# Unnormalized first chunks behind each norm, with the norm factor applied at the PSUM read, and another order of the attention heads

## The reference

```python
def rms_norm(h, gain):
    h32 = h32 * lax.rsqrt(jnp.mean(h32 * h32, axis=-1, keepdims=True) + EPS)
    return h32 * gain
...
c_act = jax.nn.silu(c)
mod = (c_act @ ada_w[layer] + ada_b[layer])          # shift, scale, gate of each sublayer
h = rms_norm(x, norm_g[layer, 0]) * (1.0 + scale) + shift
x = x + 0.5 * gate * swiglu(h, ffn_w_in[layer, 0], ffn_w_down[layer, 0])
h = rms_norm(x, norm_g[layer, 1]) * (1.0 + scale) + shift
x = x + gate * diff_attention(h, ...)                # layer 1: hgrn2(h, ...)
...
x = x + sliding_window_attention(rmsnorm(x, norm_mix[0]), ...)
x = x + peer_ffn(rmsnorm(x, norm_ffn[0]), ...)       # 16384 experts, product keys
x = x + short_gated_conv(rmsnorm(x, norm_mix[1]), ...)
x = x + peer_ffn(rmsnorm(x, norm_ffn[1]), ...)
```

## Time and profile before

| what | value |
|---|---|
| median of 3 runs | 3052.91 us (3051.86 to 3061.36) |
| the profiled execution | 3055.0 us |
| its span, first to last instruction | 3053.2 us |
| TensorE busy (matmul) | 2964.3 us, 97% |
| DVE busy | 2141.4 us, 70% |
| ACT busy | 1357.4 us, 44% |
| GpSimd busy | 569.8 us, 19% |
| mean granted TensorE clock | 0.987 |

### The profile page before, as it was taken

The page is one execution under the profiler, slowest core; times in us unless marked ns, Lnnn a source line. Parts: engine busy times, 40 slices in busy tenths (PEclk is TensorE's granted clock), DMA queues, the critical chain, the costliest instruction groups (busy, mean ns, idle before and its releaser), DMA issues.

```text
span 3053.2 us, 48385 instructions
## 1 busy us (share of the span) xinstructions
PE 2964.3 (97%) x18778; PEld 2640.5 (86%) x18778; DVE 2141.4 (70%) x3120; ACT 1357.4 (44%) x1486; POOL 569.8 (19%) x311
## 2 busy tenths in 40 slices
PE   5999899999999999999999999999999999999999
PEld 4888788888898887789999988788889999988887
DVE  7787778888766755559967755565859967755565
ACT  4444544454534444444444444444444444444443
POOL 2310313032120210008820000000008830000000
PEclk9999999999999999999999999999999999999999
DMA  7786157777633654145557656676444556655685
GB/s 299 278 284 235 70 207 275 276 269 274 233 112 136 232 171 151 42 145 187 179 200 236 236 197 219 235 280 228 166 180 167 184 199 237 231 206 208 244 288 198
DMA packets 147044, 640.58 MB, mean 210 GB/s; under 512 B 12456, under 2 KB 46416, under 8 KB 90464
## 3 DMA queue, kind: packets, MB, share of 16 engines
q1 hardware_dynamic: 127104, 568.02, 52.3%
q10 hardware_dynamic: 19808, 70.79, 6.3%
HBM read 604.14 MB, written 34.62 MB: 209 GB/s over the span
## 4 chain that ended last, share of the span: by engine, by line
PE 64%; DVE 2%; DMA 1%; ACT 1%; issue 1%; DVEq 0%; ACTq 0%
PE pp L555 10%; PE pp L1139 8%; PE pp L1140 8%; PE pp L1141 8%; PE mz L1205 7%; PE mz L1208 7%; PE mz L1207 7%; PE pp L557 5%; PE mz L1181 2%; DMA raw<-expert_v 1%; ACT w_hi L1268 1%; PE mz L515 1%; PE mz L528 0%; PE pp L1024 0%; DVE w_lo L1774 0%
## 5 line engine op out<-in xcount | busy, mean ns | idle before, releaser
L1774 DVE TENSOR_TENSOR w_lo<-raw,w_hi 128x2048 fp32r<-128x2048 f32 (+1 forms) x416 | 911.5, 2191 | 456.8 <-ACT w_hi L1268 455.9
L1268 ACT ACTIVATE w_hi<-raw 128x2048 fp32r<-128x2048 f32 (+1 forms) x486 | 893.8, 1840 | 513.7 <-DMA raw<-expert_v 362.8
L555 PE MATMUL pp<-hs,w_hi 128*128 128x512 f32 x2272 | 810.1, 401 | 21.6 <-POOL hs L2569 12.8
L557 PE MATMUL pp<-hs,w_lo 128*128 128x256 f32 x2272 | 637.6, 281 | 0.0
L1139 PE MATMUL pp<-hs,w_hi 128*128 128x256 f32 x2048 | 584.8, 286 | 0.0
L1140 PE MATMUL pp<-hs,w_hi 128*128 128x256 f32 x2048 | 579.3, 283 | 0.0
L1141 PE MATMUL pp<-hs,w_lo 128*128 128x256 f32 x2048 | 579.1, 283 | 0.0
L555 PEld LDWEIGHTS pp<-hs,w_hi 128*128 128x128 f32 x2272 | 430.3, 189 | 132.2 <-issue 13.5
L2512 POOL TENSOR_TENSOR w_lo<-raw,w_hi 128x2048 fp32r<-128x2048 f32 x64 | 319.7, 5007 | 1051.6 <-ACT w_hi L1268 1051.5
L557 PEld LDWEIGHTS pp<-hs,w_lo 128*128 128x128 f32 x2272 | 432.1, 190 | 0.9 <-issue 0.7
L1205 PE MATMUL mz<-w_hi,w_split 128*128 128x512 f32 x1024 | 401.2, 392 | 10.2 <-DVE w_split L2345 10.0
(11 more groups left out here) (309 smaller groups left out, 3270.0 us busy)
## 6 DMA issues: line engine op xcount, KB each, us to landing
raw<-expert_u SPq DMA_DIRECT2D x128, 1024.0 KB, 4.8
raw<-expert_v SPq DMA_DIRECT2D x128, 1024.0 KB, 4.8
raw<-ffn_in SPq DMA_DIRECT2D x88, 1024.0 KB, 4.9
ada_raw<-ada ACTq DMA_DIRECT2D x116, 512.0 KB, 5.3
raw<-ffn_down SPq DMA_DIRECT2D x64, 704.0 KB, 5.3
raw<-out_w SPq DMA_DIRECT2D x16, 1024.0 KB, 4.7
raw<-hgrn SPq DMA_DIRECT2D x16, 1024.0 KB, 4.8
raw<-query SPq DMA_DIRECT2D x16, 1024.0 KB, 4.8
```

Of the source, the lines that this page charges most:

```text
L555: mm(outp, w_hi[:, slot, a:a + P], rhs[:, k0 + k].rearrange("p a t -> p (a t)"), start=(k0 + k == 0), stop=False, skip_group_check=True)
L557: last = mm(outp[:, 0:T], w_lo[:, slot, a:a + P], rhs[:, k0 + k, 0, :], start=False, stop=(k0 + k == last_k), skip_group_check=True)
L1268: f(w_hi[:, slot, 0:n], raw[:, slot, 0:n], ACT.Copy).then_inc(hi_ready, 1)
L1774: v.tensor_tensor(w_lo[:, slot, 0:n], raw[:, slot, 0:n], w_hi[:, slot, 0:n].bitcast(F32), ALU.subtract)\
```

## The change

For the norms n = 1 to 9 the first two pairs of chunks (`RAW_PAIRS = 2`, four chunks) are multiplied with x times gain, without the factor 1/rms of the token. The product is multiplied by that factor when it is read from PSUM. So these four chunks do not wait for the norm.

- New operand `xs`, 516 columns a k: [low of x*gain | 2 shift columns | high of x*gain | 2 shift columns]. ACT makes the high part (`raw_high`), DVE the low part (`raw_low`), as soon as each k of x is done; DVE writes the shift columns (`shift_columns`, 8 small linked instructions for n = 1, 4 for the others).
- The raw product has three matmuls for each k where there were two (`raw_part`), of 258, 256 and 258 columns for n below 6, and of 256 each from n = 6 on.
- The first pair (`raw_pair`) is ordered by what is ready behind each kind of sublayer, with `sums` and `spread_norm` between its parts. All `keep_warm` calls of `sums`, the five in `spread_keys` and the three in sliding-window `turn` are gone. The three in `turn` of differential attention stay.
- Reading: `take_raw` on DVE replaces `take_cross` on ACT and `add_halves`. For n below 6 the shift is summed from the two columns first and added afterwards (in the ffn by the silu bias and the product that follow).
- The old `norm` chain (`h32`, `hs` high and low) moves behind: four k after chunk 1 is read and four after chunk 2 (`norm_behind`). The third pair needs `hs`.
- DVE and ACT split both chunks of the second pair before chunk 0 is read.
- `MOD_PLAN` gets a first pair: ffn_in 1 and 2 start one pair later (10 pairs, not 11), ffn_in 3 two pairs later, attention has 4 pairs instead of 3.
- In sliding-window attention step h becomes score(h+2), turn(h), weigh(h-1) on TensorE; weights(h), low(h-2), soft(h+2) on DVE; turned(h), high(h-1), expo(h+2) on ACT.
- Buffers move; `pick_sb` is loaded after the first sliding-window pair on SyncE's queue; the copy to `iota_rep` moves from ffn 0 to the first peer sublayer; the conv taps run three chunks later; the down and out products are unrolled on DVE and ACT.

```diff
+    def raw_part(n, outp, slot, tile0, k):
+        a = (tile0 + k) * P
+        more = 2 if n < 6 else 0
+        wh, wl, x_ = w_hi[:, slot, a:a + P], w_lo[:, slot, a:a + P], xs_of(n, k)
+        mm(outp[:, 0:T + more], wh, x_[:, 0:T + more], start=(k == 0), stop=False, ...)
+        mm(outp[:, 0:T], wh, x_[:, T + 2:2 * T + 2], start=False, stop=False, ...)
+        return mm(outp[:, 0:T + more], wl, x_[:, T + 2:2 * T + 2 + more], start=False, stop=(k == KD - 1), ...)
...
+    def behind_down():
+        late = 1 - half
+        pe.wait_ge(x_done, x0 + KD - 1)
+        for k in range(2): ...            # 6 parts, all tiles but (late, 0)
+        sums(n, KD - 1, KD)
+        pe.wait_ge(x_done, x0 + KD)
+        ...                               # 2 parts, then k = 2 of all 4 tiles
+        spread_norm(n)
+        parts(0, (3,)); parts(1, (3,))
+        for j in range(2):
+            parts(j, range(4, KD)).then_inc(w_used, 1)
+    def behind_out():
+        pe.wait_ge(x_done, x0 + KD - 2)
+        parts(0, range(4)); sums(n, 4, 6); parts(0, (4, 5))
+        pe.wait_ge(x_done, x0 + KD)
+        parts(1, range(2)); sums(n, 6, KD); parts(1, (2, 3))
+        spread_norm(n)
+        parts(1, (4, 5))
+        for j in range(2):
+            parts(j, (6, 7)).then_inc(w_used, 1)
+    def behind_experts():
+        for b in range(4):
+            pe.wait_ge(x_done, x0 + 2 * b + 2)
+            ...                           # k = 2b, 2b+1 of the b tiles already begun
+            if b == 3:
+                sums(n, 0, KD)
+            ...                           # tile b, k = 0 to 2b+1; at b == 3 spread_norm after k == 3
...
     # ACT
+    def norm(n, a, ph):
         for k in range(a, KD, 2):
+            squares(n, k, w)
+            raw_high(n, k) ...
         act.wait_ge(norm_sum, n + 1)
         f(inv_rms[:], mz[:, 0, 0:TB], ACT.Sqrt, ...).then_inc(norm_rms, 1)
+        split_next(ph, 0, ph.pair0, ph.pair0 % 2, ph.pair0 // 2, 0)
+        act.wait_ge(norm_wide, n + 1)
+        f(inv_w[:], mz[:, 0, T:2 * T], ACT.Copy).then_inc(inv_ready, 1)
...
     # DVE
+    def take_raw(ph, n, c, dst):
+        dve.wait_ge(inv_ready, n)
+        dve.wait_ge(w_used, 2 * ph.pair0 + c + 1)
+        if n < 6:
+            link(v.tensor_reduce(shift[:, j], pp[:, j, :, T:T + 2], AX.X, ALU.add))
+        last = v.tensor_tensor(dst, pp[:, j, :, 0:T], inv_w[:].unsqueeze(1).to_broadcast([P, 2, T]), ALU.mult)
+        if n < 6 and ph.kind != "ffn_in":
+            ...                           # two tensor_scalar that add the shift
+        last.then_inc(evac_done, 1)
...
     # sliding-window attention, TensorE
     for h in range(HEADS):
-        turn(h)
         if h + 2 < HEADS:
             score(h + 2)
-        weigh(h)
+        turn(h)
+        if h:
+            weigh(h - 1)
+    weigh(HEADS - 1)
```

More of the change, by code:

```diff
@@ L158, in beyond_plan @@
 def beyond_plan(ph, rp):
-    n = MOD_PLAN[(ph.kind, ph.index)][1]
-    return rp >= n if isinstance(rp, int) else ph.kind == "ffn_in" and n < ph.pairs
+    first, n = MOD_PLAN[(ph.kind, ph.index)][1:]
+    return not first <= rp < first + n if isinstance(rp, int) else ph.kind == "ffn_in" and first + n < ph.pairs
 def each_pair(ph):
@@ L332, in build, with xs_of @@
         one = small[:, 60:61]
+        shift = small[:, 64:68].rearrange("p (j t) -> p j t", j=2)
+        def xs_of(n, k):
+            return xs_1[:, k - 5] if n == 1 and k > 4 else xs[:, k]
         pp = psum("pp", [P, 2, 2, 512])
@@ L561, in first_pair, with raw_tile, normed_tile, wait_k @@
+            def raw_tile(ph, n, rp, pair, half, j, t):
+                for k in range(KD):
+                    last = raw_part(n, pp[:, j, t], 2 * half + j, t * KD, k)
+                return last
+            def normed_tile(n):
+                def wait_k(k):
+                    pe.wait_ge(hs_ready, KD * n + k + 1)
+                return wait_k
             def first_pair(ph, n):
@@ L599, in products @@
                         for t in range(2):
-                            last = tile_product(pp[:, j, t], 2 * half + j, t * KD, hs, 0, KD, KD - 1)
+                            last = raw_tile(ph, n, rp, pair, half, j, t)
+                        last.then_inc(w_used, 1)
+                for rp, pair, half, lap in pairs_of(pe, ph.part(raw, ph.pairs - raw)):
+                    for j in range(2):
+                        pe.wait_ge(lo_ready, 2 * pair + j + 1)
+                        pe.wait_ge(evac_done, ph.evac0 + 2 * rp + j - 1)
+                        first = isinstance(rp, int) and rp == raw and j == 0
+                        for t in range(2):
+                            last = tile_product(pp[:, j, t], 2 * half + j, t * KD, hs, 0, KD, KD - 1,
+                                                normed_tile(n) if first and t == 0 else None)
                         last.then_inc(w_used, 1)
@@ L1352, in ffn @@
                 load_modulation(ph, 0, 0)
-                for rp, pair, half, lap in itertools.chain(pairs_of(act, ph.part(0, 6)), pairs_of(act, ph.part(6, 2))):
+                for rp, pair, half, lap in each_pair(ph):
                     for j in range(2):
@@ L1356, in ffn @@
                         load_modulation(ph, 2 * rp + j + 1, 1 - j)
-                        if j == 0 and not (isinstance(rp, int) and rp == 0):
+                        if j == 0 and rp:
                             squares(n + 1, rp - 1, 1)
+                        if j and rp > 3:
+                            for k in range(2 * rp - 8, 2 * rp - 6) if rp < 7 else (6,):
+                                raw_high(n + 1, k)
             def diff_attention():
@@ L2483, in _ @@
             peer(0, 7)
-            norm(8)
+            norm(8, KD - 2)
             short_conv()
```

494 lines of the change are left out of this document (342 added, 152 removed).

## The result

The changed kernel takes 3037.7 us (median of 6 executions, 3035.4 to 3040.4) where the kernel before, on the same chip, takes 3052.4: a ratio of 0.9941, with a 95% interval of 0.9924 to 0.9957. It is faster, by 15 to 18 us. Timed again in another series it took 3039.2 against 3053.5: 0.9958, 0.9941 to 0.9975. The forecast was 3027.8, range 2998 to 3050: sign and range hold, the gain came out 7 to 10 us smaller. The profiled execution has a span of 3035.2 us against 3053.2, with a mean granted clock of 0.985 against 0.987.

A forecast was written before the change was run, and what follows sets the result against it. TensorE, in work 97% of the span, was taken as the bound. 3055.0 less 18.4 at the norms and 6.7 in the head steps gave 3029.9 profiled, median 3027.8; own range 3012 to 3042, with rivals 2998 to 3050.

The forecast's parts named there:

- Raw products start at once, and take 0.36 a k: At norm boundaries: raw parts start 0.1 us behind the last down product; three matmuls take 0.360 us a k.
- Rival D: Raw products: 258-column matmuls cost more than 256, making the kernel slower, about 3380 us at the float32 fillers' rate; chance 0.08.
- Pair 0 of nine norms, 33.4 net: Last product to end of first raw pair, nine norms: 33.4 us won, with the wait for `take_raw(0)` included.
- Second pair, 3.7: Second raw pair at nine norms: three matmuls a k cost 0.4 us more at each, 3.7 in all.
- VectorE late for the third pair, 10.3: Third pair: TensorE waits on VectorE's queue, 4.5 us at norm 1, 1.9, 1.0, 2.5, 0.4 at norms 2 to 5.
- Head steps, 6.7: Window attention: steps of 4.2 us instead of 6.04 and no first fillers win 13.7, less 7.0 for low clock: 6.7 us.
- the slow steps: Window attention's head steps: two run at 1.2 GHz, about 7.7 us a step, costing 3.5 us more each.
- Rival B: Window attention: the clock stays low through the head steps, giving 3046 us; chance 0.12.
- two more modulation chunks cost 1 later: Differential attention, norm 1: two further chunks with conditioning on VectorE cost 1 us later.
- Rivals A: Norm boundaries and heads: DVE and ACT keep up and the clock returns at once, 2999 us; chance 0.12.
- C: Norm boundaries: DVE's lateness is double what was followed, 22 us more wait, about 3050 us; chance 0.10.
- E: Norm boundaries: the first pair starts no sooner, its operands or `lo_ready` being late, about 3049 us; chance 0.03.

The follow-up runs named there:

- the two fastest: Changed kernel with attention's chunk 6 and 7 tiles behind the head loop, chunk 0 read earlier at norms 7, 8, 9: 3026.5 us; also with convolution taps sooner: 3021.1 us.
- the kernel with the other opcode: Changed kernel with the small add of each conditioning step written as scalar_tensor_tensor instead of tensor_tensor: 3038.7 us against 3052.7 for the kernel before, 0.9951.

## Why the prediction was right, and where it was not

- **Raw products start at once, and take 0.36 a k.** Right. In the first profile the mean step is 0.361 with 258 columns and 0.358 with 256; timeline rows of TensorE after, six steps of the one apart, then ten of the other:

```profile
619.45 0.28 PE L569 MATMUL pp<-xs,w_hi 128*128 128x258 f32 x1
...
621.62 0.28 PE L569 MATMUL pp<-xs,w_hi 128*128 128x258 f32 x1
...
1307.22 0.28 PE L569 MATMUL pp<-xs,w_hi 128*128 128x256 f32 x1
...
1310.80 0.28 PE L569 MATMUL pp<-xs,w_hi 128*128 128x256 f32 x1
```

  Rival D, the dear 258 columns, falls: two columns and an odd start cost 3 ns at most. Against the two-matmul step beside them (0.347 or 0.353) a raw step costs 5 to 14 ns more, so the rows' 13 was a price at the upper end. By the formula that the Trainium skill (TensorE: Matmul & The Clock Gate, Back-to-back issue gap) gives for a matmul in isolation it would be some 3; the traces show more.
- **Pair 0 of nine norms, 33.4 net.** Right: 36.3 and 33.6. The waits for `take_raw(0)` were 1.22, 1.22, 1.09, 1.09 (1.6 forecast) and 3.95 (4.4).
- **Second pair, 3.7.** It lost 4.7 and 5.9. The excess is norm 8, with 2.0 and 3.0 where 0.4 was forecast: behind its wait at chunk 2 the granted clock is 0.50 for part of the pair in both profiles, and it lost only 0.5 in the three kernels whose wait there is 1.75 us or less.
- **VectorE late for the third pair, 10.3.** Right in sum (9.6, 8.6), not norm by norm: norm 1 was given 4.5 and lost 2.4, norm 5 was given 0.4 and lost 1.7.
- **Head steps, 6.7.** Too small by 3 to 4 us. The step at full clock was right (4.24). The term that was mis-sized is that of the slow steps: 5.35 us each in the first profile and not 7.7, so that two cost 2.2 us beyond full speed (3.2 in the second profile) and not 7. Rival B falls too: without any filler the clock is full 0.9 to 3.1 us behind the start of the first `weigh`. Whether `turn` had a part in that, no run here shows.
- **The failed step: "two more modulation chunks cost 1 later".** From chunk 7 on they cost 8.3 us in the first profile and 4.7 in the second. The tiles stood at a place where they delay the keys of the first score; their instructions have both inputs in SBUF and stood still while GpSimd's split ran, which I had not looked at; so TensorE waited 5.35 us, and its clock fell in that wait. The experiments show each of the first two apart. For the clock there is the count of traces only: low in seven of seven with the wait, full in six of six without. How long it stays low is not set by the wait, and makes the difference between 4.7 and 8.3.
- **A step left out.** The taps of the convolution are not in the prediction's sum, nor among what it costed at nothing. Three of them moved into the chunks with the gating: 2.1 us of waits.
- **Rivals A, C and E** fall: the waits came, their sum was as followed, and the pair started at once.
- **Partly luck.** The total came within the range also because two errors have opposite signs: the heads gave 3 to 4 us more than forecast, while attention and convolution, with steps that the sum had wrong or left out, took 9 to 11 us more.

## What to carry to other kernels

Work that is moved to an engine "with room" must be followed in that engine's queue to the next thing another engine needs, and beside the work of the third engine that its instructions cannot overlap: here four tiles of 1.2 us cost 5 to 8 us, and nothing at all sixty microseconds later, where the engine had stood idle. When an engine sets the pace over several chunks, removing one wait only moves it; look for the chunk where it has caught up. To read differences of 2 us in a kernel of 3000, number the steps that both kernels share and follow their difference.

## What was unexpected of the hardware

**Two rates of a k step.** A plain step of two matmuls takes either 0.3467 or 0.3533 us, for whole stages at a time. Timeline rows of TensorE in ffn 1, eleven steps apart, in the first profile of the changed kernel:

```profile
480.08 0.39 PE L558 MATMUL pp<-hs,w_hi 128*128 128x512 f32 x1
...
483.89 0.40 PE L558 MATMUL pp<-hs,w_hi 128*128 128x512 f32 x1
```

and in its second:

```profile
480.24 0.40 PE L558 MATMUL pp<-hs,w_hi 128*128 128x512 f32 x1
...
484.13 0.40 PE L558 MATMUL pp<-hs,w_hi 128*128 128x512 f32 x1
```

3.81 and 3.89 us. Over the 352 steps of an ffn's first product that is 2.3 us. The same program has them in different stages in its two profiles; what decides it is open.

**The clock is about half of the noise.** TensorE's granted clock falls to 0.50, mostly for 3.4 or 6.8 us at a time, and for 17 to 27 us around the first head steps of the window attention. In windows of 1 us, I counted 67 to 94 us of it in the traces of this study; 80 in the kernel before, 89 and 87 in the two of the changed one, 70 and 71 in the two fastest. Some dips lie behind waits, others in the midst of products without any (from 1158.5 us on in the first profile of the changed kernel), and not at the same places in two executions. At half speed each microsecond costs half of one, so by this estimate 27 us more or less are some 13 us of time; a low stretch inside a wait costs less, as in attention above. Single executions of one kernel lie further apart (3028 to 3049 for the kernel with the other opcode, whose own profile has the fewest). Every execution has its mean clock on record: over the 129 that stand in series of five and more, taken against the mean of their series, a clock higher by 0.001 goes with 2.2 us less, with a correlation of -0.68. That accounts for about half of the scatter; the two rates of a k step may be a part of the rest.
